# The order of three products per row tile: from a fixed sequence to one that runs back and forth

## The reference

```python
def swiglu(h, w_gate, w_up, w_down):
    return (jax.nn.silu(h @ w_gate) * (h @ w_up)) @ w_down

def layer(x, st_h, st_conv, st_gla, reset_first, p):
    h = rmsnorm(x, p['norm_pre'][0])
    x = x + 0.5 * rmsnorm(swiglu(h, p['w_ffn_gate'][0], p['w_ffn_up'][0], p['w_ffn_down'][0]), p['norm_post'][0])
    h = rmsnorm(x, p['norm_pre'][1])
    m, h_last, new_conv, S_fin = mixer(h, st_h, st_conv, st_gla, reset_first, p)
    x = x + rmsnorm(m, p['norm_post'][1])
    h = rmsnorm(x, p['norm_pre'][2])
    x = x + 0.5 * rmsnorm(swiglu(h, p['w_ffn_gate'][1], p['w_ffn_up'][1], p['w_ffn_down'][1]), p['norm_post'][2])
    return x, h_last, new_conv, S_fin
```

## Time and profile before

| | |
|---|---|
| median of 3 runs | 2124.98 us (2123.95 to 2125.14) |
| the profiled execution | 2123.84 us |
| its span, first to last instruction | 2121.8 us |
| PE busy | 2112.5 us, 17197 matmuls |
| DVE busy | 1442.3 us |
| ACT busy | 1291.8 us |
| POOL busy | 710.0 us |

### The profile page before, as it was taken

How to read it: one execution, slowest core, us unless ns; L and a number is a source line. 1 busy time by engine, 2 the same in 40 slices (tenths; PEclk the granted TensorE clock), 3 DMA queues, 4 the chain that set the end, 5 groups by cost and what they waited for, 6 DMA issues and landing times.

```text
span 2121.8 us, 41190 instructions
## 1 busy us (share of the span) xinstructions
PE 2112.5 (100%) x17197; PEld 2087.8 (98%) x17197; DVE 1442.3 (68%) x1902; ACT 1291.8 (61%) x1989; POOL 710.0 (33%) x708
## 2 busy tenths in 40 slices
PE   9999999999999999999999999999999999999999
PEld 9999999999999999999999999999999999999998
DVE  7555857778986658845584558577689867576454
ACT  8544657658786657653564456576587765575444
POOL 3112512525654225511250124124275533152112
PEclk9999999999999999999999999999999999999999
DMA  7555555445554565555555555554465544655553
GB/s 259 168 166 164 169 180 157 150 144 175 170 159 140 151 186 164 169 168 165 167 168 168 167 164 167 179 159 142 143 191 158 155 146 152 183 167 169 166 172 129
DMA packets 100552, 350.98 MB, mean 165 GB/s; under 512 B 11409, under 2 KB 12305, under 8 KB 100369
## 3 DMA queue, kind: packets, MB, share of 16 engines
q1 hardware_dynamic: 99936, 347.68, 53.7%
q10 hardware_dynamic: 432, 0.68, 0.1%
HBM read 343.45 MB, written 4.87 MB: 164 GB/s over the span
## 4 chain that ended last, share of the span: by engine, by line
PE 96%; DVE 1%; POOL 1%; issue 1%; DMA 0%; ACT 0%; SPq 0%; DVEq 0%; POOLq 0%; ACTq 0%
PE psD L519 91%; PE psM L612 1%; POOL ssum L1652 1%; PE psM L519 0%; DVE val L1508 0%; PE psM L653 0%; PE psM L725 0%; DVE ring L1183 0%; DMA raw_ring<-in_w_gu 0%; PE psM L688 0%; POOL hidden_pair L1853 0%; PE psS L539 0%; PE psM L732 0%; PE psD L505 0%; PE psM L592 0%
## 5 line engine op out<-in xcount | busy, mean ns | idle before, releaser
L519 PE MATMUL psD<-operand,ring 128*128 128x288 f32 x10992 | 1461.1, 294 | 1.0 <-DVE operand L1251 1.0
L519 PEld LDWEIGHTS psD<-operand,ring 128*128 128x128 f32 x10992 | 1442.9, 188 | 8.7 <-issue 3.7
L1183 DVE TENSOR_TENSOR ring<-raw_ring,ring 128x1024 fp32r<-128x1024 f32 (+2 forms) x656 | 824.3, 1257 | 107.8 <-ACT ring L839 107.2
L839 ACT ACTIVATE ring<-raw_ring 128x1024 fp32r<-128x1024 f32 (+2 forms) x656 | 671.9, 1027 | 94.1 <-DMA raw_ring<-in_w_gu 47.1
L519 PE MATMUL psD<-hidden_pair,ring 128*128 128x288 f32 x4224 | 564.0, 294 | 0.9 <-POOL hidden_pair L1853 0.9
L519 PEld LDWEIGHTS psD<-hidden_pair,ring 128*128 128x128 f32 x4224 | 555.0, 188 | 5.4 <-POOL hidden_pair L1853 4.1
L1853 POOL TENSOR_TENSOR hidden_pair<-hid,hidden_pair 128x288 fp32r<-128x288 f32 x176 | 214.3, 1217 | 876.1 <-ACT hidden_pair L1127 876.1
L1127 ACT ACTIVATE hidden_pair<-hid 128x288 fp32r<-128x288 f32 x176 | 77.9, 443 | 241.2 <-DVE hid L1189 241.1
L1652 POOL TENSOR_TENSOR ssum<-ssum,sq 128x288 f32<-128x288 f32 x145 | 166.2, 1146 | 157.5 <-ACT sq L853 154.5
L1123 ACT ACTIVATE act<-gate 128x288 f32<-128x288 f32 x176 | 78.3, 445 | 225.7 <-DVE gate L1189 225.1
L1189 DVE TENSOR_TENSOR hid<-psD,act 128x288 f32<-128x288 f32 x174 | 79.1, 455 | 190.0 <-PE psD L519 183.0
(11 more groups left out here) (240 smaller groups left out, 1206.6 us busy)
## 6 DMA issues: line engine op xcount, KB each, us to landing
raw_ring<-in_w_gu SPq DMA_DIRECT2D x351, 512.0 KB, 3.6
raw_ring<-in_w_d SPq DMA_DIRECT2D x128, 448.0 KB, 3.3
raw_ring<-in_w_in SPq DMA_DIRECT2D x80, 512.0 KB, 3.6
raw_ring<-in_w_d SPq DMA_DIRECT2D x64, 512.0 KB, 3.6
raw_ring<-in_w_out SPq DMA_DIRECT2D x32, 512.0 KB, 3.6
x<-in_xT SPq DMA_DIRECT2D x8, 288.0 KB, 6.9
gates<-in_w_ax SPq DMA_DIRECT2D x4, 512.0 KB, 4.5
S<-in_st_gla SPq DMA_DIRECT2D x4, 512.0 KB, 4.6
```

The lines of the kernel that those rows point to most:

```text
L519: mm = e.matmul(out, w[:, kt * P:(kt + 1) * P], t[:, kt, :], start=(kt == 0 and part == 0), stop=(kt == KT - 1 and part == 2))
L839: e.activation(wh[u % RING][:, part], raw[u % RING][:, part], ACT.Copy).then_inc(hi_ready, 1)
L1183: e.tensor_tensor(wl[u % RING][:, part], raw[u % RING][:, part], wh[u % RING][:, part].bitcast(F32), ALU.subtract).then_inc(lo_ready, 1)
```

## The change

Within a row tile the three matmuls get another order, and every second tile the reverse of it. At even `kt`: low-high, high-high, high-low (weight by operand). At odd `kt`: high-low, high-high, low-high. What is multiplied, where it accumulates, the waits and the number of matmuls are as before. Units 1 to 3 (L502 to L510) are left as they are.

```diff
-                for part, (w, t) in enumerate([(w_h, xh), (w_h, xl), (w_l, xh)]):
+                order = [(w_l, xh), (w_h, xh), (w_h, xl)]
+                for part, (w, t) in enumerate(order[::-1] if kt % 2 else order):
                     mm = e.matmul(out, w[:, kt * P:(kt + 1) * P], t[:, kt, :],
                                   start=(kt == 0 and part == 0), stop=(kt == KT - 1 and part == 2))
```

## The result

The changed kernel takes 2153.12 us (median of 4 runs, 2152.29 to 2154.14) against 2124.54 us for the kernel before beside it: a ratio of 1.0138, 95% interval 1.0125 to 1.0150. It is slower by 29 us. The forecast was 2114 us and faster; the time lies 3 us outside the range.

A forecast was written before the change was run, and what follows sets the result against it. The prediction took TensorE's own pace as the bound: 0.7 ns less on each of 15288 products gives 10.7 us less, waits 0, issue 0. The forecast was 2114 us, its own range 2108 to 2120, the full range 2098 to 2150.

The forecast's parts named there:

- What bounds the kernel: Whole kernel: only TensorE's own pace counts, PE busy 2112.5 of 2121.8 us; DVE, ACT and POOL have slack.
- factor of 15.3 us per ns: Products of L519: one ns per product over 15288 products is 15.3 us.
- Waits, bank and ring releases cost nothing: Waits ahead of each tile's products, releases at unit ends: unchanged by the new order, 0 us.
- I take 130.0 for the new order: Products of L519: new order runs at 130.0 ns instead of a mean of 130.7, 10.7 us less.
- -0.7 ns per product: Products of L519: the forecast gain, 0.7 x 15.3 = 10.7 us less.
- fewer changes of kind leave less to trip over: Steps between products: weight and stream kinds each change at 2 of 6 steps, not 4; reason given for 130.0.
- The range: Whole kernel: from 2098 us (128.9 ns) to 2150 us (132.3 ns), with some 0.15 left outside.
- the rows of L505 and L508: Units 1 to 3: steadier sequences at 131.9 and 132.5 ns, taken as the upper bound for the new order.
- The price of the steady sequences: Rival: steps where the weight keeps its kind cost 131.9 to 132.5 ns; +23 us, 2148; chance 0.18.
- No effect: Rival: order is indifferent, side work sets the mixture of cadences; 2121 to 2129 us, middle 2125; chance 0.20.
- The rule of the Trainium skill: TensorE's two independent read ports: loading weights takes nothing from the running matmul, so order can't matter.
- The prediction's 122.5 ns: Distance between products of 288 columns, estimated from the skill page's N / 2.4 + 2.5 ns; the trace disagreed.

The follow-up runs named there:

- all-high: High weights by high operand three times per row tile, low parts left out, against the kernel before: 2146.8 us.
- e9: Kernel before (old order) with operand tiles laid out as eight high then eight low, same place modulo 256; hidden_pair unchanged: 2131.13 us.
- e10: Changed kernel with operand tiles laid out as eight high then eight low, same place modulo 256; hidden_pair unchanged: 2136.62 us.
- e3: Kernel before with its order of products reversed at odd row tiles: 2123.74 us.
- e11: Changed kernel's sequence of streamed tiles with high weights in all three products, low weights left out: 2154.01 us.
- e7: Kernel before (old order) with the weights' ring moved by 16 bytes (LEAD 32 for 28): 2145.28 us.
- e13: Kernel before with operand tiles, hidden_pair and weights' ring all moved by 32 bytes: 2124.45 us.
- e6: Changed kernel with the weights' ring moved by 16 bytes (LEAD 32 for 28): 2151.6 us.
- e1: Low-high, high-high, high-low at every row tile without reversal, against the kernel before: 2119.16 us, ratio 0.9979.

## Why the prediction was wrong

**What bounds the kernel: right.** It is PE's own pace, and the 10 ns above the stream of 288 columns is all that the change touches. The two numbers of after, 1.98 ns per product and 30.3 us of span, agree through the factor of 15.3 us per ns.

**Waits, bank and ring releases cost nothing: right.** The loads' waits on the ring went from 1.1 to 2.5 us, one wait of 2.1 us, far below the 30.

**"I take 130.0 for the new order": the step that failed.** The sum had -0.7 ns per product for a term that measured +2.0. One premise was misread: 130.0 is not the cadence of the longest undisturbed stretches as such. Of the four longest in the kernel before, the one of 1536 products runs at 130.0, the two of 1248 at 131.1, and the one of 1368 at both. The reason given, that fewer changes of kind leave less to trip over, is not borne out: all-high, without any change, costs 132.2 ns, and the kernel before, which changes the kind of weight and of stream at 4 of 6 steps each, 130.0 to 131.1. What sets the price in its place is the sequence of the streamed tiles' places, seen from the weights' place: with high and low tile at one place the two orders cost the same (131.2 ns, e9 and e10). Nor do weights of a kind matter (e3, e11). The new order also does not settle in one cadence; it has at least 131.7 and 133.3.

**The range: too short by 3 us.** Its upper end, 132.3 ns, came from the rows of L505 and L508, taken as if no order could cost more than the dearest one seen. The changed kernel spends about half of its time at 133.3 (236 of 500 pieces of 24 products). Those rows did point to the right side, and were overruled by an argument with no row behind it.

**The rivals.** The price of the steady sequences (2148 us, 0.18) came nearest in size, but its mechanism fell: it blamed the steps at which the weight keeps its kind, and the old order reversed at odd tiles has as many of them as the changed kernel (4 in 6), at a span within 0.1 us of before (e3). "No effect" fell with the result itself, +1.4%. The rule of the Trainium skill beside it, in "TensorE: Matmul & The Clock Gate", Part 2, is that TensorE reads the stream and the weights through two independent ports, and that loading the next weights takes no read bandwidth from the running matmul. The conclusion that the prediction drew from it, that order can't matter, does not hold for this kernel, and the place of the weights matters too: moving the weights by 16 bytes cost 22 us with the stream untouched (e7), and moving both by 32 bytes cost nothing that one run can tell (e13). The prediction's 122.5 ns took that page's formula further than the page does: its section "Back-to-back issue gap" gives the formula for the isolated gap, and says that in a stream of weight loads and matmuls both set the distance. Whether the two reads collide in the memory, or meet elsewhere, no run here shows.

**A question that the trace had posed.** One text at two cadences was noted, and then used as a coin to be won. The traces show that it is no coin. The kernels issue their 17197 matmuls in the same sequence of units and side work, so stretches can be matched by count. Of the 33 stretches of 96 products or more that no other matmul breaks, 31 run at the same one of the two cadences (the median over pieces of 24) in the kernel before and in the old order with both moved by 32 bytes, another execution. Two neighbours, four matmuls of side work apart, in the kernel before and then in that run:

```profile
324.43 12.97 PE L519 MATMUL psD<-operand,ring 128*128 128x288 f32 x96
...
337.99 12.86 PE L519 MATMUL psD<-operand,ring 128*128 128x288 f32 x96
```

```profile
325.55 12.97 PE L520 MATMUL psD<-operand,ring 128*128 128x288 f32 x96
...
339.11 12.86 PE L520 MATMUL psD<-operand,ring 128*128 128x288 f32 x96
```

The first runs at 131.1 and the second at 130.0, in both kernels: (12.97 - 12.86)/96 = 1.1 ns. With low-high first all 17 stretches that had 131.1 go to 130.0, and 6 of the 16 that had 130.0 go to 131.1. So the cadence of a stretch is bound to its place in the program and to the order, and 130.0 everywhere was not something that an order could be trusted to win. The code held the two sizes that matter, 1152 bytes to a tile and a ring that begins 28 elements late, and the prediction read neither.

**What stays open.** What inside the engine makes the cadences; what in a stretch's place in the program picks one of the two; and why low-high first, whose stream runs through the same cycle of places as the old order, spends more of its time at 130.0 (131.1 was the old one's in the earlier trace rows). The last is worth 5 us in 2124 and is the version to keep: 2119.16 us, 0.2% faster than before (0.9979, 0.9969 to 0.9989). One thing to start from: at the sharp cadences the three products of a row tile take 390.0, 393.3, 395.0, 396.7 or 400.0 ns, in steps of 1.67 ns, which is four periods of the granted 2.4 GHz. This is an estimate from the rows above, and no explanation; the old order moved by 128 bytes (132.6) does not fit it.

## What to carry to other kernels

Where TensorE is at full clock and never waits, measure the distance between starts in undisturbed stretches; if it takes several sharp values, as here, the placement of the streamed and the stationary tiles is a parameter to try, as the order of products is, and the two should be tried together. An order found good at one placement may be the worse one at another: here 128 bytes turn the sign. Tell such effects by an experiment that changes one half of the units and leaves the other as a control in the same run.

## What the runs showed of the hardware

- Products of 128x128 by 288 columns of this type, at a granted clock of 1.00, follow each other mostly at one of a few sharp distances: 130.0, 131.1, 131.7, 132.2, 133.3 or (e6) 134.4 ns over hundreds of products. No long stretch is under 130.0.
- The distance depends on the offset between the start of the streamed tile and of the weight tile: 130.0 and 131.1 at LEAD 28, 132.2 at LEAD 32 for the old order (2123 and 2145 us). Moving both by 32 bytes keeps both cadences (2124 us).
- Which of two cadences a stretch takes is repeated from execution to execution: 31 of 33 stretches agree between the kernel before and e13.
- Loading the same weights again instead of others changes nothing (e11 against the changed kernel: spans of 2152.0 and 2152.1 us). Streaming the same tile twice in a row is not dearer as such (e1: 2119 us, where the old order never does it and takes 2124).
